# Attention heads taken in pairs, and bias tables read ready-made from repeated rows in DRAM

## The chip, the core and the metric

The kernel runs on one core of a Trainium2 chip. A core has TensorE (PE, matrix products; PEld is its loading of weights), VectorE (DVE), ScalarE (ACT), GpSimd (POOL) and SyncE (SP), which only issues DMA transfers here. The metric is the device time of one execution in microseconds, the median of several runs.

## The reference, cut to what matters

Two transformer blocks run one after the other over 256 tokens of width 1024. The change touches only the first, which has two layers. Its attention has three branches, here numbered 0 to 2, and a bias table for each head:

```python
def neighbourhood_attention(q, k, v, rpb):          # branch 0: 8 heads of 64
    ...
    bias = rpb[:, dr[:, None, :, None], dc[None, :, None, :]]
    logits = s + bias
    logits = jnp.where(col_ok[:, None, :], logits, NEG_INF)
    ...
def diff_attention(q, k, v, lam, lam_init, subln_g, bias_table):   # branch 1: 4 heads, each of two
    bias = jnp.transpose(bias_table[t5_bucket(rel)], (2, 0, 1))
    p = jax.nn.softmax(s + bias, axis=-1)
    a = p[:, :, 0] - lam * p[:, :, 1]
    o = jnp.einsum('bhqk,bkhe->bqhe', a, v)
    o = rms_norm(o, subln_g) * (1.0 - lam_init)
    ...
def first_block(x, ...):                             # window_gqa is branch 2: 8 heads, 2 of keys
    for l in range(DEPTH):                           # DEPTH = 2
        x = x + 0.5 * swiglu(rms_norm(x, norm_g[l, 0]), ...)
        h = rms_norm(x, norm_g[l, 1])
        proj = h @ w_in[l]
        ya, yb, yc = neighbourhood_attention(...), diff_attention(...), window_gqa(...)
        g = jax.nn.sigmoid(h @ w_gate[l] + b_gate[l])
        merged = g0 * (ya @ w_branch[l, 0]) + g1 * (yb @ w_branch[l, 1]) + g2 * (yc @ w_branch[l, 2])
        x = x + merged @ w_o[l]
        x = x + 0.5 * swiglu(rms_norm(x, norm_g[l, 2]), ...)
```

The bias of a head depends on the distance between query and key alone. So row p of its table is one short row of numbers, shifted by p places.

## The kernel before

**Stages.** Each layer has a first feed-forward part (`ffn(l, 0)`, 11 blocks of 256 hidden columns), the projection (15 groups of columns), the mixing loop, the product with `w_o`, and a second feed-forward part. Then comes the second block, whose expert stage streams 200 MB of weights and ends the program. Activations lie transposed (features on partitions, 256 tokens along a row).

**Weights.** SP streams all weights in pieces of 512 KB in the order of `stream_plan` through six buffers `W`. A piece of the feed-forward, projection and gate weights is split into a high part by ACT (line 1324) and a rest by DVE (line 1663), and PE forms three products for each (`mm3`). A piece may be split up to three ahead of the one in use. SP asks for the next piece into a buffer when the rest of the old one is formed.

**The mixing loop** has 36 steps s, written out by hand in the same order on PE, DVE and ACT. On PE a step holds: the scores of head s (two matmuls, 64 rows deep, s < 24), one piece of the gate product (24 matmuls), from s = 12 on one tile j of the branch product (`yT` by `W`, four matmuls, all of them 24 tiles), the transposes of head s - 1's probabilities (line 937), and the product of head s - 2's transposed probabilities with V (`PT`,V, two matmuls; the output is 64 partitions wide in branches 0 and 2). Heads of branch 1 are transposed and multiplied once for two. Results go round four PSUM banks with one pair of counters (`begin`, `take`, `give`; `work_ready`, `work_free`). DVE adds the bias (1905, 1906), takes the maximum (1908), forms the rest of a weight piece, multiplies a merged tile (1921, 1923, 1925), copies the transposed probabilities (1934) and the head's output (1940, 1943), scales the gate (1960, on odd steps), normalises the probabilities (1976) and finishes the gate (1983) once ACT has done the tanh (1464). ACT forms the exponentials (1455).

**The norm of branch 1** stands at s = 18: ACT squares the outputs (1477), PE sums each head over partitions with a matrix of ones (two matmuls of 512 columns), ACT takes roots (1480), DVE inverts them on 128x512 tiles (1949) and scales (1952).

**Bias tables.** Each table starts as a short row in DRAM (`na_scr`, `t5_scr`). A DMA reads it with a shift of one more element for each partition, which gives the table upside down (`R5`, `R`); PE turns it over with a matrix `anti` and DVE copies it (1810) or adds the column mask (1813). `bias` does this for three tables in each feed-forward block from the fourth on: 12 T5 and 8 neighbourhood tables in layer 0, 8 in layer 1. SP loads `R5` and the two halves of `R` at pieces 23, 28 and 33 of the stream; for layer 1, ACT issues the two loads (1410) ahead of `ffn(0, 1)`. `R` lies over `QK`, and `R5` behind it. The adaptive weights of the second block are loaded and used beside (`ada_rows`); while the tables are being made, their first four units share one buffer.

## Time and profile before

| | us |
|---|---|
| median of 3 runs | 2165.75 |
| lowest, highest | 2164.09, 2170.45 |
| the profiled execution, its own time | 2166.41 |
| its span in the profile | 2164.6 |
| PE busy | 2062.4 (95%) |
| DVE busy | 1181.1 (55%) |
| ACT busy | 637.2 (29%) |
| layer 0: mixing loop and what follows up to its last probabilities | 322 to 479 |
| layer 1: the same | 1028 to 1186 |
| expert stage | 1676 to the end |

Stages are told by their matmuls in the timeline. A matmul of fp32 operands is two records (x4 is two matmuls); its duration holds the way through the array too, so a group costs the next start less its own start.

### The profile page before, as it was taken

The numbers are of one execution on the slowest core, as the hardware profiler recorded it, in microseconds if no ns is written. First come the engines' busy times: TensorE is split into PE (matmuls) and PEld (weight loads), VectorE is DVE, ScalarE is ACT, GpSimd is POOL, SyncE is SP. The second block draws the span as 40 slices with busy tenths as digits, with TensorE's granted clock in tenths as the row PEclk, the third lists the DMA queues.
The fourth block names the chain that finished last, engine by engine and source line by source line (L and its number), as shares of the span: only waits on it lengthen the run. The fifth ranks groups of instructions, "written<-read, shape, count | busy, mean of one in ns | idle before, by whom it ended". The sixth has DMA issues, their size and how long they took to land.

```text
span 2164.6 us, 33353 instructions
## 1 busy us (share of the span) xinstructions
PE 2062.4 (95%) x14055; PEld 1676.9 (77%) x14055; DVE 1181.1 (55%) x2009; ACT 637.2 (29%) x942; POOL 0.2 (0%) x4
## 2 busy tenths in 40 slices
PE   7999999999999999999998999979997999999997
PEld 7999998878999999999886899978765543444443
DVE  6665659773656666565987365565275422222222
ACT  4433434432433533343443243320042000000001
POOL 0000000000000000000000000000000000000000
PEclk9999999999999999999999999999989999999999
DMA  7976563226966676556322677632224799999996
GB/s 226 276 218 178 164 184 98 88 88 193 282 216 201 200 225 216 176 158 185 103 92 78 195 243 215 195 73 78 79 97 175 315 422 420 421 421 421 421 421 252
DMA packets 260676, 471.39 MB, mean 218 GB/s; under 512 B 15418, under 2 KB 221300, under 8 KB 235948
## 3 DMA queue, kind: packets, MB, share of 16 engines
q1 hardware_dynamic: 259216, 466.25, 62.8%
q10 hardware_dynamic: 1308, 2.96, 0.6%
q8 instruction: 114, 1.87, 0.4%
q14 instruction: 38, 0.31, 0.0%
HBM read 468.03 MB, written 1.13 MB: 217 GB/s over the span
## 4 chain that ended last, share of the span: by engine, by line
PE 77%; DMA 17%; DVE 4%; ACT 1%; issue 1%; SPq 0%; DVEq 0%; ACTq 0%
PE ps L652 75%; DMA ring_zone<-in_moe_w_up_dram 15%; DMA W<-in_ffn_w_gate_dram 2%; PE ps L937 1%; DVE QK L1949 1%; PE ps L1082 0%; DVE hl L1674 0%; DVE WL L1663 0%; DVE xT L1681 0%; ACT WH L1324 0%; DMA PT<-in_norm_g_dram 0%; SPq L581 0%; DVE xT L1726 0%; DVE yT L1952 0%; DVE xT L1861 0%
## 5 line engine op out<-in xcount | busy, mean ns | idle before, releaser
L1663 DVE TENSOR_TENSOR WL<-W,WH 128x1024 fp32r<-128x1024 f32 x372 | 453.0, 1223 | 337.7 <-ACT WH L1324 337.7
L652 PE MATMUL ps<-hh,WH 128*128 128x256 f32 x2128 | 608.0, 286 | 13.4 <-DVE WL L1663 7.7
L652 PE MATMUL ps<-hl,WH 128*128 128x256 f32 x2128 | 598.1, 281 | 0.0
L652 PE MATMUL ps<-hh,WL 128*128 128x256 f32 x2128 | 597.9, 281 | 0.0
L1324 ACT ACTIVATE WH<-W 128x1024 fp32r<-128x1024 f32 x372 | 391.5, 1056 | 486.3 <-PE ps L652 455.9
L652 PEld LDWEIGHTS ps<-hh,WH 128*128 128x128 f32 x2128 | 404.0, 190 | 34.0 <-issue 31.1
L652 PEld LDWEIGHTS ps<-hl,WH 128*128 128x128 f32 x2128 | 404.1, 190 | 0.2
L652 PEld LDWEIGHTS ps<-hh,WL 128*128 128x128 f32 x2128 | 403.7, 190 | 0.0
L652 PE MATMUL ps<-ring_over,XT 128*64 128x512 f32 x896 | 228.4, 595 | 30.2 <-DMA ring_zone<-in_moe_w_up_dram 13.6
L652 PEld LDWEIGHTS ps<-ring_over,XT 128*64 128x64 f32 x896 | 77.7, 137 | 174.9 <-issue 174.5
L652 PE MATMUL ps<-hid_h,WH 128*128 128x256 f32 x704 | 201.7, 287 | 0.0
L652 PE MATMUL ps<-hid_l,WH 128*128 128x256 f32 x704 | 197.0, 280 | 0.0
L652 PE MATMUL ps<-hid_h,WL 128*128 128x256 f32 x704 | 196.8, 280 | 0.0
L1596 ACT ACTIVATE sgE<-ps 128x512 f32<-128x512 f32 x16 | 9.6, 597 | 447.5 <-PE ps L652 447.5
L652 PEld LDWEIGHTS ps<-hid_h,WH 128*128 128x128 f32 x704 | 132.6, 188 | 6.3 <-issue 5.8
L652 PEld LDWEIGHTS ps<-hid_l,WH 128*128 128x128 f32 x704 | 132.7, 188 | 0.5
L652 PEld LDWEIGHTS ps<-hid_h,WL 128*128 128x128 f32 x704 | 132.5, 188 | 0.0
L2379 DVE TENSOR_TENSOR hidE<-sgE,ps 128x512 f32<-128x512 f32 x16 | 16.8, 1048 | 205.0 <-PE ps L652 205.0
L652 PE MATMUL ps<-yT,W 128*128 128x256 f32 x512 | 116.7, 381 | 0.0
L652 PE MATMUL ps<-ring_zone,hidT 128*64 128x512 f32 x512 | 113.4, 595 | 0.8 <-DVE SelT L2361 0.7
L652 PEld LDWEIGHTS ps<-yT,W 128*128 128x128 f32 x512 | 95.0, 190 | 15.0 <-issue 3.6
L652 PEld LDWEIGHTS ps<-ring_zone,hidT 128*64 128x64 f32 x512 | 37.8, 137 | 65.4 <-issue 64.0
(336 smaller groups left out, 2343.5 us busy)
## 6 DMA issues: line engine op xcount, KB each, us to landing
ring_over<-in_moe_w_gate_dram SPq DMA_DIRECT2D x64, 1024.0 KB, 20.3
ring_zone<-in_moe_w_down_dram SPq DMA_DIRECT2D x64, 1024.0 KB, 18.9
ring_over<-in_moe_w_up_dram SPq DMA_DIRECT2D x48, 1024.0 KB, 22.3
W<-in_ffn_w_gate_dram SPq DMA_DIRECT2D x88, 512.0 KB, 5.2
W<-in_ffn_w_up_dram SPq DMA_DIRECT2D x88, 512.0 KB, 4.4
W<-in_ffn_w_down_dram SPq DMA_DIRECT2D x88, 512.0 KB, 4.2
W<-in_w_in_dram SPq DMA_DIRECT2D x78, 512.0 KB, 4.0
W<-in_w_gate_dram SPq DMA_DIRECT2D x48, 512.0 KB, 3.6
```

Of the source, the lines that this page charges most:

```text
L652: ins = nc.tensor.matmul(o, lhsT, rhs, start=start, stop=stop, skip_group_check=True, **kw)
L937: ins = nc.tensor.transpose(bank[:, k * T + q * P:k * T + (q + 1) * P], S[:, u % 4, q * T + k * P:q * T + (k + 1) * P], ident)
L1324: nc.scalar.activation(high, W[:, i % RAW, :], ACT.Copy).then_inc(high_ready, 1)
L1596: nc.scalar.activation(sgE[:, :], bank, ACT.Silu).then_inc(sg_ready, 1)
L1663: v.tensor_tensor(low, W[:, i % RAW, :], high.bitcast(F32), ALU.subtract).then_inc(low_ready, 1)
L1949: give(v.reciprocal(r2, r2))
L2379: v.tensor_tensor(hidE[:, :].rearrange("p (k m) -> p m k", k=HIDDEN), by_row(sgE[:, :]), by_row(bank), ALU.mult).then_inc(work_free, 2)
```

## The change

Two things are changed at once.

**Pairs.** On even steps PE forms the scores of two heads in a row, the even one with the rows 0 to 63 of the array and the odd one with 64 to 127, into banks 2 and 3. On odd steps it multiplies two heads of branch 0 or 2 with V in a row, into partitions 0 to 63 and 64 to 127 of one bank (5), and DVE copies both at once. The transposes have one bank (4), and ACT, not DVE, copies them. Merged tiles alternate between banks 6 and 7. Each kind has its own pair of counters. The loop has 37 steps: tiles j from 8 on come one step later. The norm sums each head on 32 partitions of one bank (256 columns), ACT and DVE take root and inverse of that one 128x256 tile, and at s = 20 four matmuls that are one row deep spread the four factors into four banks, from which DVE scales.

**Tables.** SP copies the short rows within DRAM, each T5 row 128 times (`t5_rep`, 3.1 MB) and each neighbourhood row 64 times (`na_rep`, both layers, 3.7 MB), ahead of pieces 36 and 42. Read with a row step one element short of the row's length, such a copy gives the table the right way up: one load of `T5` ahead of piece 50, and 16 loads of 64 partitions into `Z` (rows of 256 B) ahead of piece 56, or from ACT's queue for layer 1. DVE adds the mask in place in the projection, c = 2 to 9 (`mask_columns`). `bias` is gone, `R` and `R5` too, and the units of the adaptive weights alternate between two buffers from the first on.

```diff
-ADA_ALONE = 4
 def ada_buffer(u):
-    return 0 if u < ADA_ALONE else u % 2
+    return u % 2
-STORE_AT, T5_AT, NA_AT = 20, 23, (28, 33)
+STORE_AT, REPEAT_AT, T5_AT, NA_AT = 20, (36, 42), 50, 56
+MIX_STEPS = 37
+NORM_SUMS, NORM_SPREAD = 18, 20
+QK_BANK, TURN_BANK, PV_BANK, MERGE_BANK = 2, 4, 5, 6
+SPREAD_BANKS = (PV_BANK, MERGE_BANK, MERGE_BANK + 1, 1)
+        def load_na(queue, l):
+            for half in range(2):
+                first = l * NA_H * NA_SHIFTS * NA_ROW + (1 - half) * P + NA_SHIFTS - 1
+                for h in range(NA_H):
+                    src = bass.AP(tensor=na_rep.tensor, offset=first + h * NA_SHIFTS * NA_ROW,
+                                  ap=[[NA_ROW - 1, NA_SHIFTS], [P, 6], [1, 64]])
+                    queue.dma_start(Z[half * 64:half * 64 + 64, h, :].rearrange("p (a n) -> p a n", a=6), src)\
+                        .then_inc(r_load, 16)
...
             def load_t5():
-                sp.wait_ge(scr, due(scr, 32))
-                src = bass.AP(tensor=t5_scr.tensor, offset=0, ap=[[1, P], [512, 12], [1, 3 * P]])
-                sp.dma_start(R5, src).then_inc(t5_load, 16)
+                sp.wait_ge(repeated, 32)
+                sp.wait_ge(setup, 2)
+                src = bass.AP(tensor=t5_rep.tensor, offset=P - 1, ap=[[511, P], [P * 512, 12], [1, 3 * P]])
+                sp.dma_start(T5[:, :, :], src).then_inc(t5_load, 16)
...
+            sp.dma_start(t5_rep, repeat_rows(t5_scr, t5_rep, 512)).then_inc(repeated, 16)
...
+            sp.dma_start(na_rep, repeat_rows(na_scr, na_rep, NA_ROW)).then_inc(repeated, 16)
...
+                def scores(s):
+                    pe.wait_ge(qk_free, 24 * l + s)
+                    for q in range(TT):
+                        for e in range(2):
...
+                            mm(ps[:, QK_BANK + e, q * T:(q + 1) * T], QK[e * 64:e * 64 + 64, qt_, q * P:(q + 1) * P],
+                               QK[e * 64:e * 64 + 64, kt_, :], True, True, then=qk_first if q else None)
...
+                def head_values(u):
...
+                    pe.wait_ge(pv_free, 12 * l + u // 2)
+                    for k in range(2):
...
+                        for e in range(2):
...
+                            mm(ps[e * 64:e * 64 + 64, PV_BANK, 0:T], V[:, k, vc:vc + 64], PT[:, e, k * T:(k + 1) * T],
+                               k == 0, k == 1, then=pv_ready if k and e else None)
...
+                    if s == NORM_SUMS:
+                        pe.wait_ge(sq_ready, due(sq_ready))
+                        for h in range(4):
+                            mm(ps[h * 32:h * 32 + 32, PV_BANK, 0:T], ones[:, 0:32], QK[:, h, :], True, True,
+                               then=dn_sums if h == 3 else None)
...
+                    if s == NORM_SPREAD:
+                        pe.wait_ge(dn_factor, l + 1)
...
+                        for h in range(4):
+                            mm(ps[:, SPREAD_BANKS[h], 0:T], ones[h * 32:h * 32 + 1, :], QK[h * 32:h * 32 + 1, 5, :],
+                               True, True, then=dn_spread)
...
+                        act.wait_ge(turned, due(turned))
+                        nc.scalar.activation(PT[:, turned_head(s) % 2, :], ps[:, TURN_BANK, :], ACT.Copy)\
+                            .then_inc(pt_ready, 1)
...
+                        v.tensor_copy(yT[:, u // 2, :], ps[:, PV_BANK, 0:T]).then_inc(pv_free, 1)
```

**PE, two steps in the middle of branch 0.** `C,S` are the transposes, `PT,V` the product with V, `QK` the scores; the rows left out are the rest of the 24 gate matmuls. Before:

```order
L937 MATMUL ps<-C,S 128x128 x4
L652 MATMUL ps<-PT,V 64x256 x2
L652 MATMUL ps<-QK 128x256 x2
L652 MATMUL ps<-hh,WH 128x256
L652 MATMUL ps<-hl,WH 128x256
L652 MATMUL ps<-hh,WL 128x256
...
L937 MATMUL ps<-C,S 128x128 x4
L652 MATMUL ps<-PT,V 64x256 x2
```

and now:

```order
L692 MATMUL ps<-PT,V 64x256 x4
L992 MATMUL ps<-C,S 128x128 x4
L692 MATMUL ps<-QK 128x256 x4
L692 MATMUL ps<-hh,WH 128x256
L692 MATMUL ps<-hl,WH 128x256
L692 MATMUL ps<-hh,WL 128x256
...
L992 MATMUL ps<-C,S 128x128 x4
```

Scores and products with V stand in groups of four matmuls on every second step, where they stood in twos on every step.

**DVE, one odd step at the start of the loop.** Before:

```order
L1663 TENSOR_TENSOR WL<-W,WH 128x1024
L1934 COPY PT<-ps 128x512
L1960 TENSOR_TENSOR gT<-ps,rstd 128x512
L1966 RECIPROCAL rc<-sm 128x2
L1976 TENSOR_SCALAR S<-S,rc 128x256 x2
L1983 TENSOR_SCALAR gT<-gT 128x512
```

and now:

```order
L1942 TENSOR_REDUCE mx<-S 128x2
L1947 TENSOR_SCALAR nm<-mx 128x2
L1695 TENSOR_TENSOR WL<-W,WH 128x1024
L1985 TENSOR_TENSOR gT<-ps,rstd 128x512
L1991 RECIPROCAL rc<-sm 128x2
L2001 TENSOR_SCALAR S<-S,rc 128x256 x2
L2008 TENSOR_SCALAR gT<-gT 128x512
```

The copy of the transposed probabilities is gone from DVE; all else keeps its order.

**SP, the stream from piece 34 to the end of the first feed-forward part.** `t_rep` is `t5_rep`. Before:

```order
L610 DMA QK<-na_scr 64x8x704
L581 DMA W<-in_ffn_w_down_dram 128x1024
L543 DMA ada_a<-in_w_ada_dram 128x4x256 x2
L581 DMA W<-in_ffn_w_gate_dram 128x4x256 x2
L581 DMA W<-in_ffn_w_up_dram 128x4x256 x2
L581 DMA W<-in_ffn_w_down_dram 128x1024 x2
```

and now:

```order
L659 DMA t_rep<-t_scr 1536x1x512
L618 DMA W<-in_ffn_w_up_dram 128x4x256 x2
L618 DMA W<-in_ffn_w_down_dram 128x1024 x2
L618 DMA W<-in_ffn_w_gate_dram 128x4x256 x2
L661 DMA na_rep<-na_scr 1024x1x896
L618 DMA W<-in_ffn_w_up_dram 128x4x256 x2
L618 DMA W<-in_ffn_w_down_dram 128x1024 x2
L580 DMA ada_a<-in_w_ada_dram 128x4x256 x2
L618 DMA W<-in_ffn_w_gate_dram 128x4x256 x2
L618 DMA W<-in_ffn_w_up_dram 128x4x256 x2
L647 DMA T<-t_rep 128x12x384
```

The three loads of shifted rows among pieces 23 to 33 are gone; two copies and 17 loads stand among pieces 36 to 56, each with weight pieces behind it on the same queue.

## Rows read from the trace of the kernel before

**Rows 1.** The page: the span, and busy time of each engine

```profile
span 2164.6 us, 33353 instructions
PE 2062.4 (95%) x14055; PEld 1676.9 (77%) x14055; DVE 1181.1 (55%) x2009; ACT 637.2 (29%) x942; POOL 0.2 (0%) x4
```

**Rows 2.** Waits of PE: who waited for whom: us in all, times, longest us

```profile
PE ps L937 <- DVE S L1976: 8.3, 4, 3.7
PE ps L652 <- ACT QK L1477: 3.2, 2, 1.6
PE ps L652 <- DVE S L1827: 1.9, 1, 1.9
```

**Rows 3.** Windows: from:to, us, PE, PEld, DVE, ACT, POOL busy, PEclk, DMA share, GB/s

```profile
344.70:355.72 11.02, 11.02 (x75) 8.82 (x74) 9.92 (x22) 5.01 (x13) 0.00 (x0) 1.00 0.31 97
427.00:479.00 52.00, 46.27 (x257) 35.33 (x256) 41.94 (x86) 20.30 (x51) 0.00 (x0) 0.97 0.27 88
555.00:565.00 10.00, 7.91 (x66) 7.54 (x65) 6.35 (x9) 4.95 (x5) 0.00 (x0) 1.00 0.99 332
134.00:144.00 10.00, 10.00 (x83) 8.49 (x82) 7.81 (x11) 2.78 (x3) 0.00 (x0) 1.00 0.46 144
```

**Rows 4.** Timeline of PE, two heads of branch 0: start us, us, instruction

```profile
345.98 0.60 PE L937 MATMUL ps<-C,S 128*128 128x128 f32 x4
346.51 1.08 PE L652 MATMUL ps<-PT,V 128*64 128x256 f32 x4
347.52 1.13 PE L652 MATMUL ps<-QK 64*128 64x256 f32 x4
351.49 0.60 PE L937 MATMUL ps<-C,S 128*128 128x128 f32 x4
```

**Rows 5.** Timeline of DVE, the copies in one step of branch 0

```profile
347.43 0.69 DVE L1934 COPY PT<-ps 128x512 f32<-128x512 f32 x1
348.03 0.41 DVE L1943 COPY yT<-ps 64x256 f32<-64x256 f32 x1
348.36 0.15 DVE L1966 RECIPROCAL rc<-sm 128x2 f32<-128x2 f32 x1
```

**Rows 6.** Timeline of PE, second block: scores of 512 and of 256 columns

```profile
1585.64 1.56 PE L652 MATMUL ps<-QK 64*128 64x512 f32 x4
1600.12 1.12 PE L652 MATMUL ps<-QK 64*128 64x512 f32 x4
```

**Rows 7.** Timeline of PE: eight matmuls in four column strips

```profile
96.54 1.07 PE L652 MATMUL ps<-ada_a,sc_ 128*32 128x256 f32 x16
```

**Rows 8.** Timelines of PE and DVE, the norm of the differential heads

```profile
432.12 1.98 PE L652 MATMUL ps<-QK,ones 128*128 128x512 f32 x4 [1.59 <-ACT QK L1477]
434.17 3.35 DVE L1949 RECIPROCAL QK<-QK 128x512 f32<-128x512 f32 x1 [3.19 <-PE ps L652]
```

**Rows 9.** Windows with the granted clock behind the norm, both layers

```profile
444.00:449.00 5.00, 5.00 (x21) 3.07 (x21) 4.80 (x12) 2.00 (x8) 0.00 (x0) 0.69 0.44 137
1150.00:1154.00 4.00, 4.00 (x10) 2.14 (x10) 3.87 (x8) 1.46 (x6) 0.00 (x0) 0.54 0.49 155
1154.00:1160.00 6.00, 6.00 (x34) 5.75 (x34) 4.32 (x11) 4.27 (x10) 0.00 (x0) 0.74 0.48 159
```

**Rows 10.** Timeline of PE: three T5 tables, three neighbourhood tables

```profile
97.54 2.20 PE L652 MATMUL ps<-R,C 128*128 128x384 f32 x6
158.05 2.48 PE L652 MATMUL ps<-QK,C 128*128 128x320 f32 x12
```

**Rows 11.** The page: GB/s by slice, DMA issues with KB and us to landing

```profile
GB/s 226 276 218 178 164 184 98 88 88 193 282 216 201 200 225 216 176 158 185 103 92 78 195 243 215 195 73 78 79 97 175 315 422 420 421 421 421 421 421 252
W<-in_ffn_w_down_dram SPq DMA_DIRECT2D x88, 512.0 KB, 4.2
QK<-na_scr SPq DMA_DIRECT2D x2, 1408.0 KB, 18.0
R<-t_scr SPq DMA_DIRECT2D x1, 2304.0 KB, 14.1
```

More of the change, by code:

```diff
@@ L151, with merged_tile, turned_head, value_heads @@
 LATE_BLOCK, LATE_TURNS = 1, 2
-STORE_AT, T5_AT, NA_AT = 20, 23, (28, 33)
-def bias_tables(l, i, b):
-    if i or not 3 <= b < FF_BLOCKS:
-        return []
-    tables = [("t5", h) for h in range(12)] + [("na", h) for h in range(NA_H)]
-    at = 3 * (b - 3)
-    return [t for t in tables[at:at + 3] if l == 0 or t[0] == "na"]
+STORE_AT, REPEAT_AT, T5_AT, NA_AT = 20, (36, 42), 50, 56
+NA_SHIFTS = 64
+MIX_STEPS = 37
+NORM_SUMS, NORM_SPREAD = 18, 20
+QK_BANK, TURN_BANK, PV_BANK, MERGE_BANK = 2, 4, 5, 6
+SPREAD_BANKS = (PV_BANK, MERGE_BANK, MERGE_BANK + 1, 1)
+def merged_tile(s):
+    j = s - 12 if s < NORM_SPREAD else s - 13
+    return j if 0 <= j < 24 and s != NORM_SPREAD else None
+def turned_head(s):
+    u = s - 1
+    return u if 0 <= u < 24 and (u // 8 != 1 or u % 2 == 1) else None
+def value_heads(s):
+    u = s - 2
+    return u if 0 <= u < 24 and u % 2 == 1 else None
 def stream_plan():
@@ L186, in stream_plan @@
             add("w_in", l, c)
-        for s in range(36):
+        for s in range(MIX_STEPS):
             if s < 24:
                 plan.append(("w_gate", l, s // 2, s % 2))
-            j = s - 12
-            if 0 <= j < 24 and j % 2 == 0:
+            j = merged_tile(s)
+            if j is not None and j % 2 == 0:
                 plan.append(("w_branch", l, j // 2, 0))
@@ L750, in turn_factor @@
                        then=turned_ready if tt else None)
-            def bias(l, i, b):
-                for kind, h in bias_tables(l, i, b):
-                    if h == 0 and kind == "t5":
-                        pe.wait_ge(t5_load, 16)
-                    if h == 0 and kind == "na":
-                        pe.wait_ge(r_load, 32 * (l + 1))
-                    bank = begin()
-                    if kind == "t5":
-                        mm(bank[:, 0:384], anti, R5[:, h, :], True, True, then=work_ready)
-                    else:
-                        src = R[:, h, 0:640].rearrange("p (a n) -> p a n", n=P)[:, :, 0:64]
-                        mm(bank[:, 0:320], anti, src, True, True)
-                        mm(bank[:, 320:384], anti, R[:, h, 640:704], True, True, then=work_ready)
-                    turns.step()
             def norm():
@@ L902, in _ @@
+                for s in range(MIX_STEPS):
+                    if s < 24:
+                        if s % 2 == 0:
+                            scores(s)
+                        i = s % 8
                         m = l * 12 + s // 2
@@ L932, in _ @@
                         pe.wait_ge(p_ready, due(p_ready))
-                        if u // 8 != 1 or u % 2 == 1:
-                            bank = begin()
-                            for k in range(2):
-                                for q in range(TT):
-                                    ins = nc.tensor.transpose(bank[:, k * T + q * P:k * T + (q + 1) * P],
-                                                              S[:, u % 4, q * T + k * P:q * T + (k + 1) * P], ident)
-                            ins.then_inc(work_ready, 1)
-                            t_idx[u] = turns.step()
@@ L958, in _ @@
-                    if s == 18:
-                        pe.wait_ge(sq_ready, due(sq_ready))
-                        for j in range(2):
-                            bank = begin()
-                            mm(bank[:, 0:512], ones[:, :], QK[:, 2 * j:2 * j + 2, :], True, True, then=work_ready)
-                            turns.step()
+                    if turned_head(s) is not None:
+                        if u == 0:
+                            pe.wait_ge(work_free, turns.n)
+                        else:
+                            pe.wait_ge(pt_ready, due(pt_ready))
+                        for k in range(2):
+                            for q in range(TT):
+                                ins = nc.tensor.transpose(ps[:, TURN_BANK, k * T + q * P:k * T + (q + 1) * P],
+                                                          S[:, u % 4, q * T + k * P:q * T + (k + 1) * P], ident)
+                        ins.then_inc(turned, 1)
@@ L1403, in ffn @@
                 used(2)
-            def load_na_bias(l):
-                for half in range(2):
-                    first = (l * NA_H * NA_ROWS + half) * P
-                    src = bass.AP(tensor=na_scr.tensor, offset=first, ap=[[1, 64], [NA_ROWS * P, NA_H], [1, NA_RUN]])
-                    act.dma_start(R[half * 64:half * 64 + 64, :, :], src).then_inc(r_load, 16)
             def rows(tile, at, n, src):
@@ L1442, in _ @@
                         root()
-                for s in range(36):
+                for s in range(MIX_STEPS):
                     if s < 24:
-                        turns.step()
                         b = s % 4
```

225 lines of the change are left out of this document (108 added, 117 removed).

## The prediction

> **What bounds the kernel now.** I read the page first: PE is busy 95% of the span, DVE 55%, ACT 29% [rows 1]. Next the windows by stage, since such shares are means. In a pair of steps of branch 0, 11.02 us long, PE has no idle time and DVE is busy 9.92 us; from 427 to 479 us, around the norm of branch 1, PE works only 46.27 of 52 us [rows 3]. The last row of that group is the feed-forward part: PE without a gap, DMA busy 46% at 144 GB/s. So PE sets the time up to the expert stage, and each microsecond taken off it there counts, as long as DVE in the mixing loop and DMA in the feed-forward part follow. The expert stage moves 421 GB/s in every slice [rows 11]; it starts earlier and stays as long.
>
> **Scores.** The scores of one head take PE 1.13 us with their tail, 1.05 up to the next start [rows 4]. Does a second head in the other half of the rows come free? The second block answers. Its step holds one matmul of 512 columns and one of 256, each 64 rows deep. Where both have the same rows they take 1.56 us, where they have different halves 1.12 [rows 6]: the 0.44 us between is the shorter matmul, wholly hidden. A group for two heads should then take what one took, and 12 groups for each layer go: 24 x 1.05 = 25.2 us.
>
> **Product with V.** One head takes 1.01 us (346.51 to 347.52) [rows 4]. Now two go side by side in the columns, 64 partitions each. The nearest row has four strips of 32: eight matmuls of 256 columns in 1.07 us [rows 7], as long as two alone. So 8 groups a layer go, 16 x 1.01 = 16.2 us.
>
> **The norm.** Its two sums of 512 columns take 1.98 us [rows 8]; four strips of 256 are half of [rows 7], 0.6, and the four spreading matmuls, in four row groups, I put at 0.6 too. Gain 0.7 a layer, 1.4. Its waits weigh more. PE waited 1.6 us for the squares, up to 3.7 for the probabilities that stood behind two inversions of 3.35 us on DVE, and 0.43 once at the end of the scores, in each layer: 8.3 + 3.2 = 11.5 us in all [rows 2, 8]. Now DVE inverts one tile of half the length (some 1.7 us, by 3.35 for the double), and the scaling has a step of its own. Going through steps 18 to 21 with these durations, what is late next is the squares (0.9 us, since ACT forms the exponentials first) and the first tile of branch 1 at s = 21 behind DVE's four scalings (0.4 us). 11.5 - 2 x 1.3 = 8.9 us.
>
> **The clock.** Behind that wait the granted clock was 0.69 for 5 us in layer 0, 0.54 for 4 and 0.74 for 6 in layer 1 [rows 9]: 3.1, 3.7 and 3.1 us at the lower level of 1.2 GHz, with PE busy all through, where 2.4 would have needed half. If PE hardly idles ahead of it, 9.9 / 2 = 5.0 us come back.
>
> **Bias matmuls.** Three T5 tables take 2.20 us with their tail, three neighbourhood tables 2.48 [rows 10]; without it 0.68 and 0.78 each. 12 x 0.68 + 16 x 0.78 = 20.6 us, all where PE has no gap. DVE's copies beside them go; eight mask additions come back in the projection, where DVE has room. PE also stood 1.9 us (behind DVE S L1827) when the three loads had filled the queues, and 2.1 us at 555 to 565 us in layer 1, with DMA at 0.99 [rows 2, 3]. Both go with their loads: 4.0 us.
>
> **New transfers, first feed-forward part.** In place of 2.4 + 2 x 1.4 MB, SP now moves 3.1 + 3.7 (within DRAM) + 2.4 + 1.6 MB, and the weights queue behind them. A block needs 3.15 MB of weights; at 144 GB/s for a share of 0.46, hence 313 at full share, that is 10 us. Without tables a block takes some 17.5 us (48 triples at 0.365, the gate's rate in [rows 4]), so 7.5 us a block are free. No row shows a copy within DRAM. The nearest from below is the load of shifted T5 rows, 2304 KB in 14.1 us or 167 GB/s, the nearest from above the expert stage's 421 [rows 11]. At 250, between them, the copies take 12.6 and 14.7 us; the T5 load 7.5; the Z load has 6144 rows of 256 B, between 7 us (by its bytes at the pace of the half-width load, QK<-na_scr) and 18 (if each row takes as long as one of 1 KB). How much lag can the stream bear? A piece is asked for seven to eight pieces ahead of use, some 22 us; less landing (4.2 us) [rows 11] and splitting, about 15. Step by step: lag 12.6; less 7.5, plus 14.7, 19.8, of which 5 is a stall; less 10, plus 3.3 (adaptive weights) and 7.5, 16, a stall of 1; less 7.5, plus 7 to 18. In all about 9 us lost, from 0 (copies at 421) to 22 (at 167, with the slow Z load). That `load_t5` waits for both copies costs nothing of its own, as they stand ahead in the same queue.
>
> The Trainium skill, page "DMA: Bandwidth & Descriptors", section "Latency and other measured facts", gives 207 to 214 GB/s for copies between HBM tensors; by it they would take 14.7 and 17.2 us and the stall would come to some 16 us, the time to 2105. No row here shows it.
>
> **New work for ACT.** Sixteen DMA issues ahead of `ffn(0, 1)` where two stood, at 0.3 to 0.7 us, hold back its splitting of weights by 5 to 10 us; three pieces are split ahead (some 9 us of PE work). I take 1 us, from 0 to 4. In the loop, ACT copies 20 tiles a layer at about 0.6 us; it is busy 5.01 us in a pair of 11.02 [rows 3], so this fits, but the transposes' only bank now waits for it.
>
> **Handshakes.** A pair of steps in branch 0 would be 11.02 - 1.05 - 1.01 = 8.96 us on PE. DVE falls from 9.92 us by two copies of 0.60 and one of 0.33 [rows 5] to 8.4, and it waits once or twice in each pair for the tanh or for PE (it had 1.1 us idle of 11.02). So DVE is as long as PE there. With merged tiles (s from 12) PE has 3.5 us more in each pair, and DVE is well behind. For that tightness I take 3 us; the rival below prices it fully.
>
> **Sum.** 25.2 + 16.2 + 1.4 + 8.9 + 5.0 + 20.6 + 4.0 - 9 - 1 - 3 = 68.3 us. From the profiled execution's 2166.4 that is 2098; the median of the runs, 2165.75, is the same time within 0.03%.
>
> **The rivals.**
> 1. DVE or a handshake sets the pace where no merged tile lengthens PE's step. DVE's 8.4 us plus the 1.1 us idle of today make 9.5 a pair, 0.55 over PE's 8.96; with a wait for the single score or transpose banks on top, 1. There are six such pairs a layer: 12 us in place of my 3, 2107. For it speaks DVE's 9.92 of 11.02; against it, that this idle time is partly waiting for a PE that will be faster.
> 2. The copies crowd the weights: 22 us of stall, 2111. No row excludes 167 GB/s; against it, that load shared the engines with weights, so a copy alone should be faster.
> 3. The transfers hide wholly and the waits at the norm vanish: 68.3 + 9 + 1 + 2, 2086.
> 4. The halves of the array don't overlap in the first block. The groups of four then take what two groups took, 41.4 us more: 2139. The two rows of the second block speak against it plainly.
> 5. Slower: reading 24 and 56 KB of DRAM over and over, while writing, runs far below any row. At 50 GB/s the 6.8 MB take 136 us; some 27 us fit into free time and the bearable lag, so PE stands 109 us in place of 9: 2198. It decides from about 65 GB/s: there the copies take 105 us, 78 are lost, and the gain is used up. The load of shifted T5 rows read twelve rows of 2 KB from 128 partitions just so and ran at 167 GB/s with weights behind it [rows 11], which speaks against it.
>
> The Trainium skill, page "TensorEngine Tiling (Array Packing)", section "Key Properties", says that changing the tiling mode drains the engine. It would not make a rival here: the gaps at such changes are in the durations of [rows 4], and half of the changes go.
>
> **How the numbers follow.** Forecast 50%, rival 1 14%, rival 2 16%, rival 3 10%, rival 4 5%, rival 5 5%. The range 2080 to 2120 takes in the forecast with the bounds of its stall, and rivals 1 to 3; it leaves out 4 and 5 and some spread, about 15%. Faster by over 0.3% (about what a measurement of this kernel can tell from no change, 6.5 us) is all but rival 5 and a doubt about its edge: 95%. Within 0.3% 1%, slower 4%.
>
> **What would show it.** In the mixing loop: a group of four scores (x8 records) in about 1.1 us, the same for four products with V, pairs of 9 us in branch 0 and 12 with merged tiles. At the norm: waits of PE under 1.5 us and a granted clock of 1.00. In `ffn(0, 0)`: no bias matmuls, blocks of 17.5 us, and waits of PE for WL or for W's transfers, some 9 us between 110 and 220 us. The whole is wrong if groups of four take 2 us, if the DMA share stays at 1 through the whole of `ffn(0, 0)` with PE waiting, or if PE's idle time moves into waits for DVE S or ACT PT.

## The result and the profile after

The changed kernel takes 2082.47 us (median of 4 runs, 2081.88 to 2082.91) where the kernel before, run beside it, took 2166.04: a ratio of 0.961, 95% interval 0.9595 to 0.9628. That is 83.6 us less, where 68 were forecast; the time lies inside the range, 15.6 us below the forecast. These are the page's first lines and PE's waits (us in all, times, longest) of the kernel after, beside [rows 1, 2]:

```profile
span 2080.1 us, 33242 instructions
PE 1984.5 (95%) x13991; PEld 1629.1 (78%) x13991; DVE 1132.3 (54%) x1939; ACT 655.0 (31%) x980; POOL 0.2 (0%) x4
```

```profile
PE ps L692 <- DVE WL L1695: 13.1, 2, 7.3
...
PE ps L692 <- DVE hl L1706: 5.7, 6, 1.5
...
PE ps L992 <- ACT PT L1509: 0.8, 2, 0.4
```

PE's share is still 95%: its busy time fell by 77.9 us, its idle time by 6.6. The waits of [rows 2] for the norm (8.3 and 3.2 us) are gone but for 0.8 us behind ACT's last copies. A new one has come, 7.3 us behind the split weights (WL); the other 5.8 of its 13.1 lie ahead of the first feed-forward part, as 5.6 did before. The windows of the kernel after that answer to [rows 3] (columns as there):

```profile
312.10:321.01 8.91, 8.91 (x73) 7.71 (x73) 8.38 (x19) 6.47 (x17) 0.00 (x0) 1.00 0.42 129
397.00:410.00 13.00, 12.89 (x103) 10.42 (x104) 11.35 (x25) 8.92 (x19) 0.00 (x0) 1.00 0.45 147
110.00:140.00 30.00, 30.00 (x265) 29.28 (x264) 18.69 (x22) 11.47 (x12) 0.00 (x0) 1.00 1.03 356
480.00:500.00 20.00, 12.68 (x103) 11.73 (x102) 7.52 (x10) 8.08 (x12) 0.00 (x0) 0.86 1.12 239
```

Read them in this order. A pair of steps of branch 0 takes 8.91 us, not 11.02, and PE still has no gap in it. Around the norm PE works 12.89 of 13 us at the full clock. In `ffn(0, 0)`, from 110 to 140 us, the DMA engines are full with the new transfers and PE nonetheless has no gap; over the whole of `ffn(0, 0)` from 100 us on it waits for nothing. At 480 to 500 us, the start of `ffn(0, 1)`, PE works only 12.68 of 20 us and the granted clock is lower. The timeline of PE in the kernel after shows the groups themselves, beside [rows 4, 8]:

```profile
312.10 1.13 PE L692 MATMUL ps<-QK 64*128 64x256 f32 x8
319.41 1.08 PE L692 MATMUL ps<-PT,V 128*64 128x256 f32 x8
...
397.11 0.64 PE L692 MATMUL ps<-QK,ones 128*32 128x256 f32 x8
...
408.54 0.71 PE L692 MATMUL ps<-QK,ones 1*128 1x256 f32 x8
```

Eight records of scores take 1.13 us, as four did before, and eight of the product with V 1.08, as four did. For the whole I cut both traces where DVE first updates the residual stream (`xT`) after each part. One such row of the kernel after and the one of the kernel before that answers to it, behind the first mixing loop:

```profile
459.64 0.69 DVE L1713 SCALAR_TENSOR_TENSOR xT<-ps,xT 128x512 f32<-128x512 f32 x1 [6.03 <-PE ps L692]
```

```profile
507.24 0.69 DVE L1681 SCALAR_TENSOR_TENSOR xT<-ps,xT 128x512 f32<-128x512 f32 x1 [6.03 <-PE ps L652]
```

The stretches between these cuts, in us, with the two kernels of the first experiment:

| stretch | before | after | pairs alone | tables alone |
|---|---|---|---|---|
| start to the end of `ffn(0, 0)` | 228.9 | 212.8 | 228.7 | 212.9 |
| projection, mixing loop, w_o of layer 0 | 278.3 | 246.9 | 247.0 | 278.4 |
| `ffn(0, 1)` | 220.8 | 227.7 | 221.1 | 229.8 |
| `ffn(1, 0)` | 206.6 | 200.5 | 206.7 | 200.4 |
| projection, mixing loop, w_o of layer 1 | 279.9 | 246.9 | 246.9 | 279.8 |
| `ffn(1, 1)` | 214.9 | 214.9 | 214.9 | 214.9 |
| second block and experts | 735.1 | 730.5 | 731.6 | 734.3 |

### The profile page after: what moved, and what is told of

Read it like the earlier page. It is cut to its first block, busy times and chain, and to the rows that moved or that the text cites. A ratio compares the mean times of both kernels' runs of the same rounds, so it can differ in the third digit from the quotient of the medians.

```text
span 2080.1 us, 33242 instructions
## 1 busy us (share of the span) xinstructions
PE 1984.5 (95%) x13991; PEld 1629.1 (78%) x13991; DVE 1132.3 (54%) x1939; ACT 655.0 (31%) x980; POOL 0.2 (0%) x4
## 4 chain that ended last, share of the span: by engine, by line
PE 78%; DMA 16%; DVE 3%; ACT 1%; ACTq 1%; issue 0%; SPq 0%; DVEq 0%
PE ps L692 77%; DMA ring_zone<-in_moe_w_up_dram 16%; PE ps L992 1%; ACTq L395 1%; PE ps L1128 0%; DVE hl L1706 0%; DVE xT L1713 0%; DVE WL L1695 0%; DMA PT<-in_norm_g_dram 0%; SPq L618 0%; ACT WH L1370 0%; DVE xT L1758 0%; ACT gT L1501 0%; DVE xT L1889 0%; DVE h2l L2266 0%
## 5 line engine op out<-in xcount | busy, mean ns | idle before, releaser
L692 PE MATMUL ps<-hh,WH 128*128 128x256 f32 x2128 | 604.7, 284 | 18.8 <-DVE WL L1695 13.1
L692 PE MATMUL ps<-hid_h,WH 128*128 128x256 f32 x704 | 200.5, 285 | 0.0
```

The source lines that it names most:

```text
L692: ins = nc.tensor.matmul(o, lhsT, rhs, start=start, stop=stop, skip_group_check=True, **kw)
```

## Experiments

**The two parts apart.** `pairs_only` is the kernel after with the old bias tables, `tables_only` the kernel before with the new ones. Lines that stand for the edit of `pairs_only`, against the kernel after (the rest follows from them):

```diff
-            sp.dma_start(t5_rep, repeat_rows(t5_scr, t5_rep, 512)).then_inc(repeated, 16)
...
-                    load_na(act, l + 1)
+                    load_na_bias(l + 1)
...
-                    if 2 <= c < 2 + NA_H:
-                        link(mask_columns(l, c - 2))
...
+                    bias(l, i, b)
```

and for `tables_only`, against the kernel after as well:

```diff
-                for s in range(MIX_STEPS):
+                for s in range(36):
...
-                        if s % 2 == 0:
-                            scores(s)
```

> The kernel after with the old bias tables: bias matmuls, three loads of shifted rows, two issues on ACT. Theory A, the two parts add up and the stage differences of the traces belong to the part that edits the stage: the mixing loops give their 30.0 and 31.5 us, everything else stays as in the kernel before, 2166.0 - 61.5 = 2104.5 us; the 9.0 us of old stalls and bias matmul time remain. Rival B: the small gains outside the edited stages (1.5 us twice in the projections, 4.6 us behind ffn(1, 1)) come with a loop that idles less, then 2097 us. Rival C: part of the gain in the loops needs the shorter DVE load of the new tables, then over 2110 us. PE's waits in the loops under 1 us in all by A and B.

> The kernel before with the new bias tables alone. Theory A: ffn(0, 0) -16.2, ffn(0, 1) with its sixteen issues on ACT +6.9, ffn(1, 0) -6.2, so 2166.0 - 15.5 = 2150.5 us, with the mixing loops at 184.9 and 186.4 us. Rival B: the gains of the projections and behind ffn(1, 1) belong to the tables, then 2143 us. Rival C: the ACT stall of 7.3 us is only there because the loop before is shorter, then 2143 us as well, but with no wait of PE for DVE WL at the start of ffn(0, 1).

Measured, on one chip: 2100.84 us for the pairs alone (ratio 0.971, 0.969 to 0.974) and 2147.78 us for the tables alone (0.992, 0.990 to 0.995), where the kernel before took 2162.63. So the pairs give 61.8 us and the tables 14.9, near the 61.5 and 15.5 of the two theories A; the rivals B, with 69 and 23 us, lie just outside the intervals. The table above gives the rest. Each stretch has the length of whichever kernel it shares its code with, to 0.2 us, but for two: `ffn(0, 1)` with the tables alone is 2.0 us longer still than in the kernel after (its wait is 8.8 us in place of 7.3), and the second block varies. So the parts add up (76.6 us together), and both rivals C fall: the loops gain as much with the old tables, and the wait at the start of `ffn(0, 1)` is there with the old loop too. The granted clock needs a closer look; these are windows over the start of the projection, of the kernel before (layer 0), of the kernel after (layer 0) in two executions, the second that of `after_again`, and of `sp_load` (layers 0 and 1); both are experiments below:

```profile
228.90:244.90 16.00, 14.10 (x112) 13.01 (x111) 10.11 (x17) 9.90 (x17) 0.00 (x0) 0.89 0.41 115
```

```profile
212.80:228.80 16.00, 14.10 (x122) 12.95 (x122) 10.50 (x17) 10.20 (x18) 0.00 (x0) 1.00 0.44 134
```

```profile
213.20:229.20 16.00, 14.10 (x111) 13.01 (x111) 10.07 (x17) 9.90 (x17) 0.00 (x0) 0.89 0.43 120
```

```profile
214.20:230.20 16.00, 14.10 (x112) 13.00 (x111) 10.18 (x17) 9.90 (x17) 0.00 (x0) 0.89 0.39 115
881.10:897.10 16.00, 14.09 (x123) 12.95 (x122) 10.54 (x17) 10.14 (x18) 0.00 (x0) 1.00 0.44 137
```

In all five PE idles the same 1.90 us (1.54 and then 0.36), waiting for `hl`, the low part of the layer's input, and then works without a gap. In two the granted clock stays at 1.00, in three it is 0.89, so 16 x 0.11 x 2 = 3.5 us at the lower level of 1.2 GHz, and 1.75 us of work lost. `after_again` is the kernel after itself: its stretch with the first mixing loop is 248.4 us long, for 246.9. The same goes for the second block, in 50 us from the last cut, for the kernel before, the kernel after and `sp_load`:

```profile
1429.50:1479.50 50.00, 38.81 (x186) 32.59 (x185) 27.79 (x49) 11.66 (x19) 0.00 (x0) 0.86 0.09 27
```

```profile
1349.60:1399.60 50.00, 38.81 (x197) 32.91 (x196) 29.55 (x50) 11.66 (x19) 0.00 (x0) 0.90 0.14 41
```

```profile
1342.90:1392.90 50.00, 38.81 (x185) 32.51 (x184) 27.80 (x49) 11.66 (x19) 0.00 (x0) 0.86 0.09 27
```

The stretch behind them is 735.1, 730.5 and 735.0 us long; by these rounded clocks, some 2 us of the difference arise in the windows themselves. The second trace of `sp_load`'s kernel, `sp_load_again`, has 0.90 there and 730.8 us. At the norm of layer 0, with the waits of [rows 2] unchanged, `tables_only` has a longer stretch at a low clock than [rows 9] show, and lost there what it kept in the projection:

```profile
426.00:434.00 8.00, 7.88 (x29) 5.67 (x30) 7.64 (x19) 3.32 (x9) 0.00 (x0) 0.57 0.58 197
```

So 3.0 us in the projections and 4.6 us in the second block, 7.6 of the 84.5 by which the traced execution got shorter, aren't shown to be work of the change. In the projection of layer 0 and in the second block, executions of one kernel differ by as much. In the projection of layer 1 none does: the clock is 0.89 in both traces with the old loop and 1.00 in all twelve with the new one, and the second block is long in both traces with the old loop as well, so a part of rival B stays open. I can't say what decides the clock.

**The loads on ACT's queue.** `sp_load` issues the sixteen loads of layer 1 from SP, inside the feed-forward part:

```diff
                 round_and_square(lambda k: col("norm_g", l * 24 + 16 + k), ahead=True)
-                if l + 1 < DEPTH:
-                    load_na(act, l + 1)
                 ffn(l, 1)
...
+                    if plan[i] == ("ffn_gate", (0, 1), 3, 0):
+                        load_na(sp, 1)
```

> The kernel after with the sixteen loads of layer 1 issued from SP's queue at the fourth block of ffn(0, 1), not from ACT ahead of it. Theory A, ACT's 10.8 us of issues hold up the splitting of weights: PE's wait of 7.3 us at 490 us and the lower granted clock behind it (0.94 for 60 us, 3.6 us at the lower level, so 1.8 back) go, 2082.5 - 9 = 2073.5 us, and w_o with ffn(0, 1) takes 218.7 us (227.7 in the kernel after, 220.8 before, of which 2.1 was a stall on a load). Rival B: the 14 us of issues on SP's queue stall the weights there instead, 2082 us or more, with PE waiting for W or WL inside ffn(0, 1). Rival C: the wait belongs to the change of stage and not to the issues, no difference.

> The kernel after, unchanged, timed on the same chip as the next one. All theories: the ratio on record, 0.961, again; 2082 us if the kernel before takes 2166 us.

> The kernel after with the loads of layer 1 on SP's queue, timed beside the kernel after. Theory A, the 9.5 us that its stage ffn(0, 1) was shorter in the trace (218.3 us from update to update, 227.8 in the kernel after) reach the end: 9 to 10 us less than the kernel after, ratio to before 0.957. Rival B, the 5 us that lay between the two medians on different chips are all that is left at the end, since a later stage gives some back: ratio 0.959. Each traced stage but ffn(0, 1) within 1.5 us of the kernel after by A.

First what ACT did in the kernel after, from its timeline (ACTq rows are the issues):

```profile
483.29 0.66 ACTq L395 DMA_DIRECT2D Z<-na_rep  x1
...
483.98 10.72 ACTq L395 DMA_DIRECT2D Z<-na_rep  x12
494.80 4.11 ACT L1370 ACTIVATE WH<-W 128x1024 fp32r<-128x1024 f32 x4 [10.80 <-issue]
```

The last twelve issues take 10.72 us: most of them 0.65, one 1.89 and one 1.84. All sixteen run from 481.02 to 494.7, and only then does ACT split the next piece of weights. PE is at the lower level for 4.2 us when it starts again, which costs 2.1:

```profile
497.17:501.40 4.23, 4.23 (x20) 4.23 (x21) 3.35 (x3) 3.19 (x4) 0.00 (x0) 0.50 0.79 251
```

The windows of `sp_load_again` over that place, to be set beside 480:500 of the kernel after:

```profile
480.00:500.00 20.00, 20.00 (x174) 19.13 (x173) 13.61 (x17) 12.86 (x17) 0.00 (x0) 1.00 0.92 301
500.00:520.00 20.00, 20.00 (x179) 19.28 (x179) 13.15 (x16) 8.35 (x9) 0.00 (x0) 1.00 0.91 188
```

PE has no gap and the full clock; SP issues the same loads in 11.0 us (from 506.8 to 517.9), with weights asked for ahead of them, and PE waits for nothing in the whole part, so rival B falls. `ffn(0, 1)` takes 218.2 us in both traces of this version, against 227.7 and 228.0 in the two of the kernel after: theory A, 9.5 us, of which 7.3 are the wait and 2.1 the lower clock behind it. The edit moves the loads to another queue and to a later place at once; that ACT's queue alone is to blame is read from its idle time of 10.80 us, no run separates the two. At the end: `sp_load` 2076.32 us (ratio 0.959, 0.957 to 0.961; theory A said 2073.5); on a second chip `sp_load_again` 2073.26 us (0.958, 0.956 to 0.960) beside `after_again` at 2088.43 (0.964, 0.962 to 0.967). The kernel after was thus slower against the kernel before than on record. Its five runs there are 2083.05, 2083.30, 2088.43, 2088.98 and 2089.41 us, in two groups 5.8 us apart; its four runs on record were all near the lower group. Those of `sp_load_again` are 2071.36 to 2073.49 and one of 2079.18. The gap has the size of the differences in the projections and the second block: the two traces of `sp_load`'s kernel, 2077.9 and 2071.5 us long, differ by 1.4 us in the first of these places and 4.2 in the second. (No run of the upper group of the kernel after was traced.) By the medians `sp_load_again` is 15.2 us ahead of `after_again`, fastest against fastest 11.7, by the traced spans 10.0 (2081.5 against 2071.5), which is what theory A of `sp_load_again` expected; its ratio of 0.958 lies between A's 0.957 and B's 0.959 and doesn't decide. This version beats both kernels.

**The copies within DRAM.** `copies_alone` makes SP wait for each copy (first fence); `copies_x3` makes the second one three times:

```diff
             sp.dma_start(t5_rep, repeat_rows(t5_scr, t5_rep, 512)).then_inc(repeated, 16)
+            sp.wait_ge(repeated, 16)
...
             sp.dma_start(na_rep, repeat_rows(na_scr, na_rep, NA_ROW)).then_inc(repeated, 16)
+            sp.wait_ge(repeated, 32)
```

```diff
             sp.dma_start(na_rep, repeat_rows(na_scr, na_rep, NA_ROW)).then_inc(repeated, 16)
+            for other in more:
+                sp.dma_start(other, repeat_rows(na_scr, other, NA_ROW)).then_inc(repeated, 16)
...
-                sp.wait_ge(repeated, 32)
+                sp.wait_ge(repeated, 64)
```

> The kernel after, with SP waiting behind each of the two copies within DRAM until it has landed, so that nothing new is asked for beside it. The copies of 3.1 and 3.7 MB then show their own duration. At the 350 GB/s and more that the slices of the kernel after show: some 9 and 10.5 us with 2 us of start each. At the 250 GB/s of the prediction: 12.6 and 14.7 us. At the 207 to 214 GB/s that the Trainium skill, page DMA: Bandwidth & Descriptors, section Latency and other measured facts, gives: 14.7 and 17.2 us. PE: if the queue bears the 15 us of lag that the prediction worked out and 7.5 us come back in each block, no stall in the first two cases and up to 2 us in the third.

> The kernel after, with the copy of the neighbourhood rows made three times in a row (two of them into scratch that nobody reads), the load of the T5 rows behind all of them. At the 307 GB/s that the copy of the T5 rows shows where nothing runs beside it (104 to 112 us of the run with the copies alone), each further copy keeps the weights away for 12 us, 24 us more. Theory A, the queue of pieces bears a lag of 15 us, as the prediction had it, and some 7.5 us come back in each block: PE stalls for 20 us or more, 2103 us. Rival B, it bears the whole 22 us of asked pieces and the copies share the engines with the weights, so that weights land beside them: a stall of 5 to 12 us, 2088 to 2095 us. Rival C, weights that are asked for later overtake the copies: under 2 us.

SP's timeline and windows in `copies_alone`:

```profile
100.26 0.88 SPq L659 DMA_DIRECT2D t_rep<-t_scr  x1
115.06 1.27 SPq L618 DMA_DIRECT2D W<-in_ffn_w_up_dram  x2
...
118.43 1.02 SPq L662 DMA_DIRECT2D na_rep<-na_scr  x1
137.00 0.92 SPq L618 DMA_DIRECT2D W<-in_ffn_w_up_dram  x2
```

```profile
104.00:106.00 2.00, 2.00 (x20) 2.00 (x19) 1.04 (x1) 0.47 (x1) 0.00 (x0) 1.00 0.79 300
...
110.00:112.00 2.00, 2.00 (x19) 2.00 (x19) 1.23 (x1) 1.33 (x2) 0.00 (x0) 1.00 0.79 307
```

From issue to the next issue, 14.8 and 18.6 us pass, but the first part of each is spent on weights asked for before: the rate of a copy with nothing beside it is the 300 to 307 GB/s of the windows, so 10.2 us for 3.1 MB and, by the same rate, 12.0 us for 3.7 MB; the second copy has no stretch of its own in the trace. That is neither the prediction's 250 nor the 350 of windows where weights move beside it. The time is 2084.29 us. The Trainium skill, page "DMA: Bandwidth & Descriptors", section "Latency and other measured facts", has 207 to 214 GB/s for its copies of tiles between HBM tensors, where the row pitch is 512 KiB or padded; the windows here show 40 to 48% more. What SP waited for (us in all, times, longest) between 90 and 220 us:

```profile
SPq L618 <- DMA na_rep<-na_scr: 15.8, 1, 15.8
SPq L618 <- DMA t_rep<-t_scr: 12.8, 1, 12.8
```

In that stretch PE waited 0.2 us for weights, though SP asked for nothing for 12.8 and 15.8 us: no stall to speak of, as expected at this rate. With three copies, windows and PE's one wait:

```profile
126.00:140.00 14.00, 14.00 (x128) 13.29 (x127) 6.42 (x8) 3.56 (x4) 0.00 (x0) 1.00 1.01 322
140.00:158.20 18.20, 3.10 (x27) 2.89 (x25) 0.00 (x0) 0.00 (x0) 0.00 (x0) 0.66 0.99 317
```

```profile
162.50 0.55 PE L696 MATMUL ps<-hh,WH 128*128 128x256 f32 x1 [19.40 <-DVE WL L1699]
```

The time is 2104.67 us, near theory A's 2103, and the stall of 19.4 us is just under its 20. Three copies of 3.67 MB at 320 GB/s are 34.4 us, and some 2.7 us were left of the first copy's lag (10.2 less the 7.5 that a block gives back): 37.1 less a stall of 19.4 is 17.7 us that the asked pieces bear. The prediction's 15 was near. Rivals B and C, with stalls of 5 to 12 and under 2 us, fall: queued copies push the weights back, and nothing overtakes them. That they do so one for one went into the 17.7 and isn't a finding of its own.

**Halves of the array.** Three edits of the groups. `same_half` lets both heads of a group read the same 64 rows, and so leaves out the odd heads' scores:

```diff
-                            mm(ps[:, QK_BANK + e, q * T:(q + 1) * T], QK[e * 64:e * 64 + 64, qt_, q * P:(q + 1) * P],
-                               QK[e * 64:e * 64 + 64, kt_, :], True, True, then=qk_first if q else None)
+                            mm(ps[:, QK_BANK + e, q * T:(q + 1) * T], QK[0:64, qt_, q * P:(q + 1) * P],
+                               QK[0:64, kt_, :], True, True, then=qk_first if q else None)
```

`scores_in_turn`:

```diff
-                    for q in range(TT):
-                        for e in range(2):
+                    for e in range(2):
+                        for q in range(TT):
```

`products_in_turn`, for branches 0 and 2:

```diff
-                    for k in range(2):
-                        for e in range(2):
+                    for e in range(2):
+                        for k in range(2):
```

> The kernel after, where the scores of the second head of each group read the same 64 rows as those of the first (so the odd heads get the even heads' scores; what they should compute is left out). Number, size and order of the matmuls are unchanged. Theory A, the second head comes free because it lies in the other half of the rows: now a group of four lasts as long as four matmuls of 256 columns one behind the other, 0.86 us more (two at some 0.43, from the starts 0.216 us apart of their two passes), 24 groups, 21 us in all, each mixing loop 10.3 us longer. Rival B, a part of the gain is that there are fewer groups with their starts and tails: the group lasts under 2 us but the whole costs less than the 25.2 us of the prediction's term by that part. Rival C, no difference.

> The kernel after, with the four scores of a group in the order head, query tile (a head's two matmuls behind each other) in place of query tile, head. Nothing else moves. Theory A, two matmuls in different halves of the rows overlap only where they stand next to each other: in the order of the kernel after the group holds two such pairs and lasts as two matmuls, here only its middle two can overlap and it lasts as three, 0.4 to 0.5 us more; 24 groups, 10 to 12 us, each mixing loop with w_o 5 to 6 us longer than 246.8 us from update to update. Rival B, the engine takes up work for a free half whatever stands between: no difference. Rival C, the gain of the scores came from fewer groups and their tails and not from halves that overlap: no difference either, but then a group of four scores lasts as long as two groups before.

> The kernel after, with the four products with V of branches 0 and 2 in the order head, key tile in place of key tile, head; branch 1 is untouched. Theory A, as for the scores, now with two halves of the columns: 0.4 to 0.5 us more in each of the 8 groups of a layer, 3 to 4 us a layer, 7 us in all. Rival B: no difference.

The groups in PE's timelines, of `same_half` and of `scores_in_turn`:

```profile
321.82 1.99 PE L692 MATMUL ps<-QK 64*128 64x256 f32 x8
```

```profile
321.80 1.14 PE L692 MATMUL ps<-QK 64*128 64x256 f32 x8
```

With both heads in one half, a group takes 0.86 us more and each loop 256.9 us in place of 246.9: 20.1 us in all, theory A's 21. (2101.31 us at the end.) So 20.1 us of the scores' gain is overlap of the two halves, shown; whether the 5.1 us up to the prediction's 25.2 are there too, as rival B has it, isn't. For the products no run put both heads in one half: only their group of 1.08 us shows that overlap. The order inside a group, though, makes no difference: the loops take 246.9 and 246.9 us with the scores in turn, 247.0 and 247.0 with the products in turn (2083.33 and 2081.21 us at the end). My theory A of these two runs is wrong: a group lasts no longer when two matmuls of the first half stand ahead of the second half's. Rival B fits; rival C, that the halves don't overlap, is out by `same_half`. The Trainium skill, page "TensorEngine Tiling (Array Packing)", section "Key Properties", says that "Tiles operate independently"; these two runs agree: what is in the order between them doesn't matter over two matmuls.

**The norm.** `norm_slow` puts the long inversions back, on tiles that nobody reads:

```diff
+                        v.reciprocal(flat(QK[:, 6:8, :]), flat(QK[:, 6:8, :]))
+                        v.reciprocal(flat(QK[:, 2:4, :]), flat(QK[:, 2:4, :]))
                         v.reciprocal(QK[:, 5, :], QK[:, 5, :]).then_inc(dn_factor, 1)
```

> The kernel after with two inversions of 128x512 (3.35 us each in the trace of the kernel before) on DVE ahead of the short one in the norm, on tiles that nobody reads any more. Theory A, the two inversions are what made PE wait and the chip lower the clock: PE waits 3 to 4 us in each layer for what stands behind them on DVE, the granted clock behind it falls to 0.5 to 0.75 for some 5 to 10 us, and each loop takes 4.5 to 6 us longer, 9 to 12 in all. Rival B, the step of its own that the scaling got hides them: under 1 us a layer and a clock of 1.00.

Its windows, and the row of PE that waited:

```profile
411.20:417.50 6.30, 0.23 (x3) 0.05 (x2) 6.14 (x9) 1.39 (x3) 0.00 (x0) 0.86 0.44 148
417.50:424.00 6.50, 6.50 (x37) 5.52 (x38) 5.62 (x17) 3.84 (x9) 0.00 (x0) 0.61 0.00 1
```

```profile
417.49 1.09 PE L992 MATMUL ps<-C,S 128*128 128x128 f32 x4 [6.07 <-ACT PT L1509]
```

2108.15 us at the end, and the loops take 10.0 and 9.1 us longer (1.5 of the first is the projection's clock); 4.2 more lie in the second block, which is 734.7 us long here, and the rest in the two feed-forward parts of layer 0. The mechanism of theory A is shown, wait and clock both: 6.07 us of waiting, and then 6.5 x 0.39 x 2 = 5.1 us at the lower level, 2.5 us of work lost. The size was too small in my expectation of 9 to 12 us in all, which took the wait of 3.7 us from [rows 2]. The timelines of DVE and ACT:

```profile
407.21 3.34 DVE L1973 RECIPROCAL QK<-QK 128x512 f32<-128x512 f32 x1
410.47 3.29 DVE L1974 RECIPROCAL QK<-QK 128x512 f32<-128x512 f32 x1
413.68 1.70 DVE L1975 RECIPROCAL QK<-QK 128x256 f32<-128x256 f32 x1
...
416.22 0.61 DVE L2003 TENSOR_SCALAR S<-S,rc 128x256 f32<-128x256 f32 x2
```

```profile
415.96 0.91 ACT L1501 ACTIVATE gT<-gT,bgh 128x256 f32<-128x256 f32 x2 [8.62 <-DVE gT L1987]
416.77 0.58 ACT L1509 ACTIVATE PT<-ps 128x512 f32<-128x512 f32 x1
```

In the faster loop 6.1 of these 6.6 us come through. Most of it is the old chain: the probabilities S that PE has to transpose are ready only at 416.8. The last half microsecond is a new one. The transposes have one bank now, ACT empties it, and its copy stands behind the tanh, which waits 8.62 us for DVE's scaled gate. Whatever delays DVE here now reaches PE through ACT as well.

**DVE as the next bound.** `copies_on_dve` gives the copies of the turned probabilities back to DVE:

```diff
-                        act.wait_ge(turned, due(turned))
-                        nc.scalar.activation(PT[:, turned_head(s) % 2, :], ps[:, TURN_BANK, :], ACT.Copy)\
-                            .then_inc(pt_ready, 1)
+                        dve.wait_ge(turned, due(turned))
+                        v.tensor_copy(PT[:, turned_head(s) % 2, :], ps[:, TURN_BANK, :]).then_inc(pt_ready, 1)
```

> The kernel after with the copies of the turned probabilities back on DVE (20 a layer, 0.69 us each by the trace of the kernel before). Theory A, DVE is the next bound of branch 0: it is busy 8.3 us or so in a pair of 8.91, with two copies 9.7, and with the 1 us that it stands idle in a pair the pair takes 10.3 to 10.7 us; over the five or six pairs ahead of the merged tiles 7 to 11 us a layer, and less behind them, where a pair is longer: 14 to 24 us in all. Rival B, DVE has room: 0 to 3 us, and only its idle time shrinks.

Windows over its second and third pair, and PE waiting in the third:

```profile
322.89:332.44 9.55, 8.99 (x74) 7.71 (x73) 9.06 (x22) 5.00 (x12) 0.00 (x0) 1.00 0.34 106
332.44:342.24 9.80, 9.14 (x73) 7.71 (x72) 9.30 (x22) 4.99 (x12) 0.00 (x0) 1.00 0.32 104
```

```profile
340.65 1.08 PE L692 MATMUL ps<-PT,V 128*64 128x256 f32 x8 [0.66 <-DVE PT L1965]
```

2096.92 us; the loops take 254.8 and 253.2 us, without the clock's 1.5 in the first 6.4 each over 246.9, 12.8 in all. DVE does become the bound, at 9.55 to 9.8 us a pair, but with 0.5 us of idle time in a pair, not the 1 us that I had added: theory A in kind, just under its lower end in size.

## Why the prediction was right, and where it was off

The forecast was 68.3 us, the traced gain 84.5. Term by term:

- **Bias matmuls, 20.6.** Held. `ffn(1, 0)` has no other edit and lost 6.2 us, for 8 x 0.78 = 6.2. The first stretch lost 16.1, for 14.4 of matmuls and the old stall of 1.9 (with the same code up to there it varies from 211.9 to 214.6 us between runs, so this one is known to some 1.5 us).
- **Old load stalls, 4.0.** Held: 1.9 there, and 2.1 in `ffn(0, 1)`, where `sp_load` takes 218.2 us for 220.8 before, 2.6 less.
- **New stall in `ffn(0, 0)`, -9.** Failed: no stall. The step that failed first is the rate of the copies, 250 GB/s between two far bounds. With the measured 10.2 and 12.0 us its own steps give a lag of 10.2 - 7.5 + 12.0 = 14.7 us, just under the 15 that it called bearable and under the 17.7 measured. So rivals 2 and 5 fall, and 9 us come to the gain. The later steps were too strict. The `Z` load kept SP's queue for 14.2 us:

```profile
156.94 14.24 SPq L395 DMA_DIRECT2D Z<-na_rep  x16
```

  With that length the steps reach 14.7 - 10 + 10.8 = 15.5 and then 15.5 - 7.5 + 14.2 = 22.2 us, which should have stalled PE by 4.5, and it didn't wait. Why not is open; from 99 to 157 us the engines moved 340 to 365 GB/s where the steps reckon with 313 and less. Two of its readings were wrong besides: the row of `QK<-na_scr`, 1408 KB in 18.0 us, gives 20 us for the bytes of the `Z` load and not 7, and its steps at 167 GB/s with a slow `Z` load add up to some 30 us of stall, not 22.
- **Issues on ACT, -1.** Failed: -9 (-9.5 by `sp_load`). The step that failed is "three pieces are split ahead (some 9 us of PE work)" as the measure of what ACT may lose. Three pieces were split, and PE had work for 8.8 us from the first issue (481.02 to 489.85). But 2.9 of these ACT needs for other work ahead of its next split (as `sp_load_again` shows), and 2.4 go by until that split and its rest are made. That leaves 3.5 us, and ACT was held for 10.8, just over the 5 to 10 forecast, so 7.3 reached PE. The clock behind that wait, for which the prediction had no term, cost 2.1.
- **Scores 25.2, products 16.2, norm 1.4, waits 8.9, clock 5.0, handshakes -3: 53.7.** Measured 61.5: the two loop stretches lost 31.5 and 33.0, of which 3.0 belong to the projections' clock. The mechanisms held: `same_half` for the scores, `norm_slow` for waits and clock, groups of 1.13 and 1.08 us. Sizes: the handshakes cost nothing (a pair of branch 0 takes 8.91 us for a sum of 8.96), 3 us; PE's waits at the norm and the tail are 0.8 in all where 2.6 were left, 1.8 us. The other 3.0 us lie in the branches behind, where a pair of branch 1 with merged tiles fell from 12.89 to 11.63 us, by 1.26 where one group of scores is 1.05; no run separated them.
- **Not forecast, 7.6.** The clock in the projections (3.0) and in the second block (4.6). All but the 1.5 us in layer 1's projection has been seen to go one way or the other in executions of one kernel.

68.3 + 9 - 8 + 7.8 + 7.6 = 84.7. The two misses of about equal size cancelled, which is luck, and half of the 16 us that remain are the clock's and for the most part luck too. `after_again`, whose median is 75.3 us below that of the kernel before, and the 76.6 us of the two parts apart suggest that the 83.6 on record are at the upper end of what this change gives.

Rival 1 fell with the kernel as it is, but narrowly: DVE is busy 8.38 of 8.91 us, and with two copies more it is the bound, at 0.6 to 0.9 us a pair over PE's 8.91 (`copies_on_dve`). Half of its 1.1 us of idle time went when PE got faster, as the prediction had argued. Rival 3 came nearest, 2086: the transfers hide wholly and the waits all but vanish. Rival 4 is excluded by the 1.13 us of the group and, from the other side, by `same_half`.

## What to carry to other kernels

Price every DMA that an engine issues as work of that engine, in the order of its queue: sixteen small loads ahead of a dependent split cost 9.5 us on ACT and nothing on SP, a few blocks later, whose pieces were already asked for. What the engine may lose is less than the work its consumer still has, by all that the engine must do before it can deliver again. A transfer that delays a stream costs only what exceeds the pieces in flight, so work out that lag before fearing the transfer, and measure it by making the transfer three times. When matmuls use half of the array's rows or columns, put two side by side in either order; the second came free here.

## What the runs showed of the hardware

- Copies from DRAM to DRAM that read 24 to 56 KB over and over ran at 300 to 322 GB/s in these windows, at a DMA share of 0.79 alone and 0.99 to 1.01 one behind the other. How the same copies would run from rows that don't repeat wasn't tried.
- The overlap of two halves of TensorE doesn't need alternating matmuls: 1.13 us alternating, 1.14 in turn, 1.99 in the same half.
- The granted clock around the same idle time of 1.54 and 0.36 us stayed at 1.00 or was 0.89 over 16 us, in two executions of the kernel after. With the second block this makes 5.6 of the 6.4 us between two traces of `sp_load`'s kernel; five runs of the kernel after spread over as much (2083.05 to 2089.41), which is two thirds of what `sp_load` gained.
- An issue of a 96 KB load on ACT's queue held it for 0.63 to 0.81 us, but twice for 1.84 and 1.89, in a stretch with the DMA share at 1.09 to 1.14.
